# Sixteen of 128 V chunks multiplied in plain fp32, in eight pairs, and eight row gathers moved from the U stretch to the V stretch

## The reference, cut to what matters

```python
s = einsum('thcd,hckd->thck', q, sub_keys)            # 8 heads, 2 x 128 keys
...                                                   # top 16 of 256 candidates for each head
u = exp_u[eidx]                                       # eidx: (tokens, 8, 16) of 16384 rows
v = exp_v[eidx]
a = gelu(einsum('td,thkd->thk', xb, u))
return einsum('thk,thkd->td', gw * a, v)
```

## Time and profile before

| | before |
|---|---|
| time, median of 3 runs | 1788.76 us (1787.02 to 1788.97) |
| the profiled execution: time, span | 1783.71 us, 1782.0 us |
| busy: PE, DVE, ACT, POOL | 98%, 73%, 37%, 24% of the span |
| weight loads (PEld) busy | 85% |
| DMA | 583.35 MB, mean 327 GB/s |

### The profile page before, as it was taken

How to read it: one execution, slowest core, us unless ns; L and a number is a source line. 1 busy time by engine, 2 the same in 40 slices (tenths; PEclk the granted TensorE clock), 3 DMA queues, 4 the chain that set the end, 5 groups by cost and what they waited for, 6 DMA issues and landing times.

```text
span 1782.0 us, 25428 instructions
## 1 busy us (share of the span) xinstructions
PE 1743.2 (98%) x10420; PEld 1517.4 (85%) x10420; DVE 1294.5 (73%) x1831; ACT 653.0 (37%) x1049; POOL 433.2 (24%) x294
## 2 busy tenths in 40 slices
PE   7999999999999999999999999999999999999996
PEld 6888888788788899999999999977777777777774
DVE  6544555558594299889544474479999899999997
ACT  5334545434543200222100011144454454554453
POOL 1000122100010002111121211124555455555440
PEclk9999999999999999999999999999999999999998
DMA  9654433656328487999999999999999999999994
GB/s 354 243 186 174 157 126 135 283 189 235 143 103 346 195 352 283 355 387 392 386 421 421 420 421 418 422 372 414 421 421 421 422 421 420 421 420 417 421 405 154
DMA packets 81859, 583.35 MB, mean 327 GB/s; under 512 B 9632, under 2 KB 9696, under 8 KB 11792
## 3 DMA queue, kind: packets, MB, share of 16 engines
q1 hardware_dynamic: 52848, 374.37, 52.7%
q0 software_dynamic: 28896, 207.36, 28.7%
HBM read 573.73 MB, written 7.34 MB: 326 GB/s over the span
## 4 chain that ended last, share of the span: by engine, by line
PE 90%; DMA 5%; DVE 3%; ACT 1%; issue 1%; SPq 0%; POOL 0%; DVEq 0%; ACTq 0%
PE bank L1021 25%; PE bank L718 11%; PE bank L735 10%; PE bank L1082 6%; PE bank L1079 6%; PE bank L1080 6%; PE bank L1071 6%; PE bank L1069 6%; PE bank L720 6%; DMA slots<-in_stream 3%; PE bank L1036 2%; PE bank L958 1%; DMA rows<-in_peer_v,eidx 1%; DMA act_raw<-in_xT 1%; PE bank L825 1%
## 5 line engine op out<-in xcount | busy, mean ns | idle before, releaser
L1021 PE MATMUL bank<-h2T,slots 128*128 128x144 f32 x3744 | 468.7, 286 | 2.8 <-DMA slots<-in_stream 2.7
L1021 PEld LDWEIGHTS bank<-h2T,slots 128*128 128x128 f32 x3744 | 462.1, 190 | 3.7 <-ACT ga L1368 3.5
L718 PE MATMUL bank<-act_split,ring_hi 128*128 128x512 f32 x896 | 320.4, 402 | 9.5 <-DVE ring_lo L1476 9.2
L1465 DVE TENSOR_TENSOR ring_lo<-ring_raw,ring_hi 128x2048 fp32r<-128x2048 f32 x90 | 205.9, 2290 | 135.4 <-ACT ring_hi L1138 135.1
L1836 DVE SCALAR_TENSOR_TENSOR rows<-rows,hrow 128x2048 f32<-128x2048 f32 x112 | 255.9, 2285 | 33.3 <-DMA hrow<-h_classes 15.1
L720 PE MATMUL bank<-act_split,ring_lo 128*128 128x256 f32 x896 | 251.5, 281 | 0.0
L689 POOL DMA_INDIRECT rows<-in_peer_v,eidx x64 | 189.5, 2960 | 168.2 <-DVE hrow L1842 144.1
L718 PEld LDWEIGHTS bank<-act_split,ring_hi 128*128 128x128 f32 x896 | 169.4, 189 | 51.1 <-DVE act_split L1476 9.5
L1138 ACT CAST ring_hi<-ring_raw 128x2048 fp32r<-128x2048 f32 x90 | 171.9, 1909 | 89.2 <-PE bank L735 72.1
L689 POOL DMA_INDIRECT rows<-in_peer_u,eidx x64 | 126.5, 1977 | 267.3 <-DVE rows L1836 266.7
L720 PEld LDWEIGHTS bank<-act_split,ring_lo 128*128 128x128 f32 x896 | 170.2, 190 | 0.1
(11 more groups left out here) (305 smaller groups left out, 2877.6 us busy)
## 6 DMA issues: line engine op xcount, KB each, us to landing
slots<-in_stream SPq DMA_DIRECT2D x213, 1024.0 KB, 11.7
ring_raw<-in_stream SPq DMA_DIRECT2D x91, 1024.0 KB, 4.9
grown<-in_stream SPq DMA_DIRECT2D x32, 1024.0 KB, 11.5
front_slots<-in_stream SPq DMA_DIRECT2D x7, 1024.0 KB, 12.6
w<-in_w SPq DMA_DIRECT2D x4, 1024.0 KB, 9.0
spill_slots<-in_stream SPq DMA_DIRECT2D x4, 1024.0 KB, 12.5
gb<-in_ln_g POOLq DMA_DIRECT2D x3, 1024.0 KB, 11.9
gb<-in_ln_b POOLq DMA_DIRECT2D x3, 1024.0 KB, 14.6
```

Of the source, the lines that this page charges most:

```text
L718: pe.matmul(bank[n % 2][:, :], hi[:, k * P:(k + 1) * P], act_split[:, k].rearrange("p c t -> p (c t)"), start=(k == 0), stop=False, skip_g ...
L1021: last = pe.matmul(bank[(N_U + k) % 2][:, 0:NU], u_slot(k)[:, ko * P:(ko + 1) * P], h2T[:, ko, :], start=(ko == 0), stop=(ko == KO - 1))
L1465: dve.tensor_tensor(ring_lo[:, r, :], ring_raw[:, r, :], ring_hi[:, r, :].bitcast(F32), ALU.subtract).then_inc(lo_ready, 1)
```

## The change

Sixteen of the 128 V chunks, in eight pairs (26 and 27, 38 and 39, and so on up to 110 and 111), aren't split. TensorE multiplies them in plain fp32, straight from the landed slot with the unsplit weights: for each block of 512 columns a product of 128 tokens for each chunk of the pair, and a rest product of 64 tokens for each, the first into PSUM partitions 0 to 63 and the second into 64 to 127 (the fold adds them). The other 112 chunks are split as before, but the weights are split for two chunks at a time. The rows done by the end of the U stretch go from 76 to 68, and the V stretch's 108 are shared out with 15 parts for a plain chunk and 7 for a split one. Some marks in the U stretch, which hang on the rows, move by 4 to 6 chunks.

```diff
-GROWS_AFTER = (11, 22)
+GROWS_AFTER = (6, 11)
...
+PLAIN = tuple(13 + 6 * i for i in range(8))
+SPLIT = [c for c in range(CHUNKS) if c // 2 not in PLAIN]
+TURN = {c: i for i, c in enumerate(SPLIT)}
+SHARE_SPLIT, SHARE_PLAIN = 7, 15
+
+def pair_end(c):
+    return (c | 1) + 1
...
-BGELU_AT, TURN_AT, FINISH_AT = 88, 91, 94
-WGELU_AT = 44
-IN_CHOICE, IN_QUADS, IN_U = 4, 28, 76
+BGELU_AT, TURN_AT, FINISH_AT = 92, 95, 98
+WGELU_AT = 50
+IN_CHOICE, IN_QUADS, IN_U = 4, 28, 68
...
-    done = in_units(CHUNKS - 1) + min(rest, rest * (m + 1) // (ENDING - 4))
+    shares = [SHARE_SPLIT if c in TURN else SHARE_PLAIN for c in range(RH, CHUNKS)]
+    done = in_units(CHUNKS - 1) + min(rest, rest * sum(shares[:m + 1]) // sum(shares[:ENDING - 4]))
...
-                    sp.wait_ge(split_used, before + 1)
+                    sp.wait_ge(split_used, before + 1 if before in TURN else pair_end(before))
...
+            def plain_pair(c):
+
+                for i in range(2):
+                    _, landing, count = raw_slot(c + i)
+                    pe.wait_ge(landing, 16 * count)
+                for j in range(NQ):
+                    cols = slice(j * 512, (j + 1) * 512)
+                    for i in range(2):
+                        pe.matmul(bank[V_BANKS[j]][:, :], weights(c + i)[:, 0:P], raw_slot(c + i)[0][:, cols], start=False,
+                                  stop=False, skip_group_check=True)
+                    for i in range(2):
+                        last = pe.matmul(bank[C_BANK + j][i * NS:(i + 1) * NS, :], weights(c + i)[:, P:ND],
+                                         raw_slot(c + i)[0][:, cols], start=False, stop=False, skip_group_check=True)
+                        if j == NQ - 1:
+                            last.then_inc(split_used, 1)
...
             for c in range(ENDING):
-                pe.wait_ge(w_ready, c + 1)
-                pe.wait_ge(split_lo, c + 1)
+                if c not in TURN:
+                    if c % 2 == 0:
+                        plain_pair(c)
+                    continue
+                pe.wait_ge(w_ready, TURN[c] // 2 + 1)
+                pe.wait_ge(split_lo, TURN[c] + 1)
...
-                    act.wait_ge(split_used, m - RH + 1)
+                    act.wait_ge(split_used, SPLIT[TURN[m] - RH] + 1)
...
-                if c >= RW:
-                    act.wait_ge(split_used, c - RW + 1)
-                act.copy(w_split[:, c % RW, W_TWICE:W_TWICE + NS], weights(c)[:, P:ND])
-                act.copy(w_split[:, c % RW, 0:ND], weights(c)).then_inc(w_hi, 1)
+                if TURN[c] >= RW:
+                    act.wait_ge(split_used, pair_end(SPLIT[TURN[c] - RW]))
+                w, r = weight_pair(c), w_at(c)
+                act.copy(w_split[:, r:r + 2, W_TWICE:W_TWICE + NS], w[:, :, P:ND])
+                act.copy(w_split[:, r:r + 2, 0:ND], w).then_inc(w_hi, 1)
...
             for m in range(CHUNKS - RH):
-                w_low(m + RH)
-                split_low(m + RH)
+                if m + RH in TURN:
+                    if (m + RH) % 2 == 0 and m + RH >= RW:
+                        w_low(m + RH)
+                    split_low(m + RH)
                 gathers(in_chunks(m))
```

More of the change, by code:

```diff
@@ L384, in weights, with weight_pair @@
             return (w_front if k < HALF else w_back)[:, k % HALF, :]
+        def weight_pair(c):
+            return (w_front if c < HALF else w_back)[:, c % HALF:c % HALF + 2, :]
         def u_slot(u):
@@ L1068, in rest_products @@
                 rest = bank[C_BANK + j]
-                pe.matmul(rest[:, :], w_split[:, c % RW, W_PAIR:W_PAIR + P], hi[:, cols], start=first, stop=False,
+                pe.matmul(rest[:, :], w_split[:, w_at(c), W_PAIR:W_PAIR + P], hi[:, cols], start=first, stop=False,
                           skip_group_check=True)
-                return pe.matmul(rest[0:NS, :], w_split[:, c % RW, P:ND], lo[:, cols], start=False, stop=final,
+                return pe.matmul(rest[0:NS, :], w_split[:, w_at(c), P:ND], lo[:, cols], start=False, stop=final,
                                  skip_group_check=True)
@@ L1078, in whole_products @@
                 whole = bank[V_BANKS[j]]
-                pe.matmul(whole[:, :], w_split[:, c % RW, 0:P], hi[:, cols], start=first, stop=False, skip_group_check=True)
-                pe.matmul(whole[:, :], w_split[:, c % RW, W_LO:W_LO + P], hi[:, cols], start=False, stop=False,
+                pe.matmul(whole[:, :], w_split[:, w_at(c), 0:P], hi[:, cols], start=first, stop=False, skip_group_check=True)
+                pe.matmul(whole[:, :], w_split[:, w_at(c), W_LO:W_LO + P], hi[:, cols], start=False, stop=False,
                           skip_group_check=True)
-                return pe.matmul(whole[:, :], w_split[:, c % RW, 0:P], lo[:, cols], start=False, stop=final,
+                return pe.matmul(whole[:, :], w_split[:, w_at(c), 0:P], lo[:, cols], start=False, stop=final,
                                  skip_group_check=True)
+            def plain_pair(c):
[12 more added lines that the diff above has]
+                            last.then_inc(split_used, 1)
             pe.wait_ge(idx_out, 2)
@@ L1105, in _ @@
                     whole_products(c, j, False, False)
-            pe.wait_ge(w_ready, CHUNKS)
-            pe.wait_ge(split_lo, CHUNKS)
+            pe.wait_ge(split_lo, TURN[last] + 1)
             for j in range(2):
@@ L1430, in _ @@
                     act.wait_ge(quad_out, DENSE_Q)
-                    for c in range(RH):
+                    for c in range(0, RW, 2):
                         w_high(c)
```

21 lines of the change are left out of this document (12 added, 9 removed).

## The result

| | before | changed |
|---|---|---|
| time, median | 1788.60 us of 4 runs (1787.02 to 1788.97) | 1802.54 us of 4 runs (1802.07 to 1803.97) |
| ratio, with its 95% interval | | 1.0090 (1.0078 to 1.0103) |
| the profiled execution: time, span | 1783.71 us, 1782.0 us | 1802.98 us, 1801.2 us |

The changed kernel is 0.9% slower. Two differences must be kept apart: 13.9 us between the medians, 19.2 us between the profiled executions, since the profiled execution of before was 3.3 us shorter than the shortest of its other runs, while that of the changed kernel lies within them.

The account below looks back on a forecast made before the run. TensorE's own pace was taken to bound V, with the DMA queues close behind; +20.0 us for plain pairs and -6.0 for U's waits made +14.0 on the median of 1788.76, so 1803 us, range 1789 to 1818.

Parts of the forecast that it names:

- The likeliest case: Whole kernel: plain pairs cost V +20.0 us, U gives back 6.0, so 1803 us, 0.8% slower; chance 0.50.
- the rival of no or part overlap: Rest products in V's pairs: column groups overlap partly, 1816.5 us, or not at all, 1830 us; chance 0.12.
- the rival that it is free: V's plain pairs: changing between whole array and column groups costs nothing, V +8.8 us, total 1791.6 us; chance 0.18.
- the sum: Forecast's addition over U and V: +20.0 us for eight plain pairs, -6.0 for U's waits, +14.0 in all.
- the rival that they run faster with a lighter VectorE: V's split products: spacing falls from 230 ns to 224.7, saving 12.8 us, total 1790 us; chance 0.08.
- U's waits: U and the change to V: eight rows fewer remove 6.0 of 6.6 us of TensorE waits; bounds 2 and 7.
- Rows in fours ... It just fits, cost 0.: VectorE at each pair: four rows through three buffers finish in time, cost 0; rows 2 us later cost 10 in all.
- DMA in V. Level: cost 0: V: twelve chunks with rows need 57.5 us of DMA against 57.8 of TensorE; cost 0, bound +5.
- Rows or chunks late: Rival in V: the run of four rows or full DMA queue costs 5 to 12 us more, 1808 to 1815; chance 0.12.

Follow-up runs that it names:

- the kernel with one group: The changed kernel with both rest products of a plain pair in the same column group (PSUM partitions 0 to 63); 1824.47 us.
- the pairs in their best order: The changed kernel with one switch into column groups per pair, rows shared evenly, V rows resumed one chunk earlier after the row weights' gelu; 1793.30 us, ratio 1.0028.

## Why the prediction came out

**What was right.** The likeliest case was forecast at 1803 us and came, and by its own mechanism for the most part. The plain passes are 0.43 us apart, the two column groups overlap (against the rival of no or part overlap, which the kernel with one group shows at +3.40 us a pair), the change of mode costs 0.35 us a block (against the rival that it is free), and a pair without waits takes 11.59 us where the sum had 11.7. The pairs alone lengthened V by 19.4 us; the sum had 20.0. The split products stayed at 230 ns, against the rival that they run faster with a lighter VectorE.

The Trainium skill ("TensorEngine Tiling (Array Packing)", Key Properties) says that a change of the tiling mode drains TensorE. The plain products agree with it, at 0.35 us in and out; the fp32r product of 64 columns shows no gap.

**U's waits.** The sum took 6.0 of 6.6 us, with 7 as the bound; 7.0 came. Moving the rows did to U what was said.

**The step that failed: "Rows in fours ... It just fits, cost 0."** It cost 4.2 us, in five of eight pairs, inside the bound of 10 that stood beside it. I had the fourth row end 17.3 us after the first one's start; it ended 18.3 after (1279.09 to 1297.4), since the gather that it hangs on came back late: 13.7 us lie between the first row's end and the fourth's start, where 12.6 were reckoned. The subtraction was ready at 21.0 us instead of 20.2, and TensorE came at 19.9 instead of 20.9, as the first row of the run itself began late. The margin of 0.7 us was smaller than the 1.1 us by which this one refill of a buffer came later than reckoned. With 19.0 us in the pairs (8 x (11.59 - 9.22)) and 4.2 behind them, 0.9 of V's 24.1 is left, about what V differs between two executions of before.

**The step that was right by its number and thin in its reason: "DMA in V. Level: cost 0".** The sum took the pairs' longer time on TensorE as given. Without them the same sum is 12 chunks with 10.7 rows, 22.7 MiB or 56.5 us of DMA against 55.3 us of TensorE, some 12 us too much over V by estimate. I did not do it. Moving eight rows left the DMA idle in U, and V had to bring them in: 17.3 us by itself, more than the 7.0 us that U gave back. In the change most of this does not show, because the pairs hold TensorE for 19 us longer, in which the gathers can catch up: with the pairs alone the DMA engines moved 408 and 404 GB/s in V's two long stretches, not the 420 of the earlier trace rows. Rows and pairs cost V 17.3 and 19.4 us alone, and 24.1 together, not their sum; in time the rows alone are 0.5% slower, the pairs alone 1.1%, both 0.9%. I had treated them as independent; the forecast held because the larger of two overlapping costs was the one worked out, and that part of it is luck.

**The 5 us.** Against the profiled execution my sum was too small: +14.0 forecast, 24.1 - 7.0 = +17.1 found, and 2.1 ahead of U. Against the medians it is 13.9. That the second agrees to 0.1 us is in part luck: the median of before lay 5 us above its profiled run, the changed kernel's did not. Where the longer runs of before spend the 5 us stays open.

**The rivals.** "Rows or chunks late" came true in part, 4.2 us of the 5 to 12; the free change of mode and the missing overlap are excluded by the experiments above, faster split products by their unchanged spacing.

## What to carry to other kernels

When two resources are level over a stage, look at the stage ahead of it before taking load away there: idle DMA time in U was paid for in V, which got 5.5 us longer for four rows and 17.3 for eight, while U gave back 6.4 and 7.0. The fastest kernels here, with 72 rows, hardly wait in U and hardly idle there (411 GB/s from 1040 to 1160 us, where 76 rows moved 420 and 68 rows 382). A saving on one engine counts only up to the next chain beside it; work out that chain (here four rows through three buffers) with its longest waits, not with the median landing time alone. Ask, too, which resource sets the stage once the edit is in: with the pairs in their best order V was as long as with the rows alone, and what the pairs cost TensorE no longer showed. Before mixing whole-array and column-group products in plain fp32, sort them so that the mode changes once.

## What the runs showed of the hardware

The fp32 products pay 0.35 us for each excursion to 64 columns and back, the fp32r product of the same shape nothing. Two fp32 products in different column groups interleave their passes completely: 1.08 us for four passes, against 1.93 in one group.

A short wait can cost more than itself: after PE stood still for 4.45 us the next 8 matmuls ran at half pace, after 3.86 us the next 14, at a granted clock of 0.53 and 0.50. The wait's length alone doesn't tell when: with one change of mode and even rows a wait of 2.75 us was followed by eight such matmuls (granted clock 0.53 from 1431.2 to 1434.6 us), and another of 2.49 us, 9 us later, by none.
